# Two stacked transformer blocks: stage ends by token tile, the root mean square on products, and unrolled layers

## The reference

```python
def first_block(x, c, ...):
    for l in range(2):
        sh1, sc1, gt1, sh2, sc2, gt2 = split(silu(c) @ w_ada[l] + b_ada[l], 6)
        u = x * (1 + sc1) + sh1
        y = mixer(u, ...)                   # w_in, attention, convolution, gates, w_out
        x = layer_norm(ALPHA * x + (1 + gt1) * y, ln_mix_g[l], ln_mix_b[l])
        u = x * (1 + sc2) + sh2
        h = square(relu(u @ w_up[l])) @ w_down[l]
        x = layer_norm(ALPHA * x + (1 + gt2) * h, ln_ffn_g[l], ln_ffn_b[l])

def second_block(x, ...):
    for l in range(2):
        h = rmsnorm(x, ln_mix_g[l])
        proj = h @ w_in[l]                  # three kinds of attention: ya, yb, yc
        gates = sigmoid(h @ w_gate[l] + b_gate[l])
        x = x + (gates[0] * (ya @ w_br_a) + gates[1] * (yb @ w_br_b) + gates[2] * (yc @ w_br_c)) @ w_o[l]
        h = rmsnorm(x, ln_ffn_g[l])
        x = x + (silu(h @ w_ffn_gate[l]) * (h @ w_ffn_up[l])) @ w_ffn_down[l]
    return rmsnorm(x, final_norm_g)
```

## Time and profile before

| | before |
|---|---|
| median of 3 runs | 2055.03 us (2049.10 to 2055.74) |
| span of the profiled execution, first to last instruction | 2034.9 us |
| TensorE busy | 1834.9 us, 90% |
| VectorE busy | 1293.3 us, 64% |
| ScalarE busy | 868.6 us, 43% |
| GpSimd busy | 48.1 us, 2% |
| DMA | 345.85 MB, mean 170 GB/s |

### The profile page before, as it was taken

How to read it: one execution, slowest core, us unless ns; L and a number is a source line. 1 busy time by engine, 2 the same in 40 slices (tenths; PEclk the granted TensorE clock), 3 DMA queues, 4 the chain that set the end, 5 groups by cost and what they waited for, 6 DMA issues and landing times.

```text
span 2034.9 us, 29393 instructions
## 1 busy us (share of the span) xinstructions
PE 1834.9 (90%) x8402; PEld 1439.7 (71%) x8402; DVE 1293.3 (64%) x2005; ACT 868.6 (43%) x1463; POOL 48.1 (2%) x96
## 2 busy tenths in 40 slices
PE   5698997999698997999499999899989999989997
PEld 2385576777475576777399777688869977768886
DVE  3468987556668986555445688645544568864554
ACT  1244333444243343444145566434435556643443
POOL 0000000000100000000100000000000000000000
PEclk9799998999799998999799999999999999999999
DMA  7675554656375544555266533445555653345553
GB/s 234 240 247 165 166 166 153 199 186 211 122 233 159 165 156 165 186 196 175 84 212 189 172 122 105 155 154 179 179 184 170 189 174 119 104 155 156 180 178 116
DMA packets 210879, 345.85 MB, mean 170 GB/s; under 512 B 20104, under 2 KB 95798, under 8 KB 210530
## 3 DMA queue, kind: packets, MB, share of 16 engines
q1 hardware_dynamic: 208756, 337.79, 52.1%
q0 software_dynamic: 2032, 6.97, 1.1%
HBM read 343.62 MB, written 1.07 MB: 169 GB/s over the span
## 4 chain that ended last, share of the span: by engine, by line
issue 50%; POOLq 1%; POOL 0%; DVE 0%
POOLq L1463 0%; POOL x_rstd L1464 0%; POOLq L1471 0%; DVE x_res L1668 0%; POOLq L1478 0%; POOLq L1298 0%; POOL sub_rstd L1464 0%; POOL lat_rstd L1464 0%; POOLq L1469 0%; POOLq L1474 0%; POOL gates L1457 0%; POOLq L1476 0%; POOLq L352 0%
## 5 line engine op out<-in xcount | busy, mean ns | idle before, releaser
L125 DVE TENSOR_TENSOR w_lo_b<-w_raw_b,w_hi_b 128x1024 fp32r<-128x1024 f32 (+3 forms) x336 | 363.0, 1101 | 195.2 <-ACT w_hi_b L119 193.2
L119 ACT CAST w_hi_b<-w_raw_b 128x1024 fp32r<-128x1024 f32 (+3 forms) x336 | 314.0, 951 | 177.2 <-PE acc_b L146 79.9
L119 ACT CAST w_hi_a<-w_raw_a 128x1024 fp32r<-128x1024 f32 x232 | 241.6, 1049 | 246.9 <-PE prod_a L146 127.2
L144 PE MATMUL prod_b<-w_hi_b,hT_hi 128*128 128x512 f32 (+1 forms) x912 | 340.5, 373 | 6.5 <-DVE hT_lo L207 3.7
L125 DVE TENSOR_TENSOR w_lo_a<-w_raw_a,w_hi_a 128x1024 fp32r<-128x1024 f32 x232 | 277.5, 1222 | 97.6 <-ACT w_hi_a L119 96.8
L146 PE MATMUL prod_b<-w_hi_b,hT_lo 128*128 128x512 f32 (+1 forms) x912 | 334.6, 367 | 0.0
L145 PE MATMUL prod_b<-w_lo_b,hT_hi 128*128 128x512 f32 (+1 forms) x912 | 333.8, 366 | 0.0
L144 PE MATMUL prod_a<-w_hi_a,uT_hi 128*128 128x512 f32 x592 | 243.4, 411 | 12.9 <-DVE uT_lo L207 7.0
L146 PE MATMUL prod_a<-w_hi_a,uT_lo 128*128 128x512 f32 x592 | 237.5, 401 | 0.0
L145 PE MATMUL prod_a<-w_lo_a,uT_hi 128*128 128x512 f32 x592 | 237.5, 401 | 0.0
L144 PEld LDWEIGHTS prod_b<-w_hi_b,hT_hi 128*128 128x128 f32 x912 | 173.2, 190 | 34.0 <-issue 5.8
(11 more groups left out here) (308 smaller groups left out, 2511.2 us busy)
## 6 DMA issues: line engine op xcount, KB each, us to landing
w_raw_a<-in_w_in_dram SPq DMA_DIRECT2D x72, 512.0 KB, 3.8
w_raw_b<-in_w_in_dram SPq DMA_DIRECT2D x192, 172.0 KB, 2.4
ada_raw<-in_w_ada_dram SPq DMA_DIRECT2D x64, 512.0 KB, 5.9
w_raw_a<-in_w_up_dram SPq DMA_DIRECT2D x64, 512.0 KB, 4.5
w_raw_a<-in_w_down_dram SPq DMA_DIRECT2D x64, 512.0 KB, 5.4
w_raw_b<-in_w_gate_dram SPq DMA_DIRECT2D x96, 256.0 KB, 3.0
w_raw_b<-in_w_ffn_gate_dram SPq DMA_DIRECT2D x88, 256.0 KB, 3.5
w_raw_b<-in_w_ffn_up_dram SPq DMA_DIRECT2D x88, 256.0 KB, 4.2
```

What stands on the lines that cost most here:

```text
L119: act.copy(self.hi[:, s, 0:cols], self.raw[:, s, 0:cols]).then_inc(self.hi_done, 1)
L125: dve.tensor_tensor(self.lo[:, s, 0:cols], self.raw[:, s, 0:cols], self.hi[:, s, 0:cols].bitcast(F32), ALU.subtract).then_inc(self.lo_done, 1)
L144: pe.matmul(out, a_hi, w_hi, start=first and c == 0, stop=False)
```

## The change

- **Tile by tile at stage ends.** A new method `part` multiplies a weight group against one token tile. The last four groups of w_out and w_o, and the last down products of both feed-forwards, run for token tile 0 first, then for tile 1. New semaphores (`down0_done`) tell VectorE that tile 0 of a down product is complete.
- **Half rows.** Residual and norm go by token tile and by half rows of 512 columns; u_ready, u2_ready and h_ready count four halves for two tiles. Transposes of a half start when that half is there.
- **Transposes between parts.** `turned_tile` runs the first weight tile of a stage tile by tile, with the turns of the later halves between its groups. In block 2 the first two turns of the next stage stand between the last parts of the stage before.
- **Block 1, next layer.** The norm's gain and shift are folded into the next layer's modulation, so u comes straight from the statistics. x itself is normed after the low parts of u.
- **Block 2.** x is multiplied by the gain alone; the reciprocal root is applied to the products (`take_scaled`, the gate sum, the tanh, and for the hidden rows half the root and its square). ScalarE's squares move behind the last high part, and ScalarE and VectorE wait for the root before they touch products.
- **Layers unrolled.** All loops over layers are loops of the program that writes the kernel; loops over weight tiles stay.

```diff
+    def part(self, pe, pos, lhs, k0, width, chunks, tok, out, first, last, tile_end=True):
+        s = pos.slot(RING)
+        lhs_hi, lhs_lo = lhs
+        if tok == 0:
+            pe.wait_ge(self.lo_done, pos.count(RING + 1))
+        for c in range(chunks):
...
+        if last and tile_end and tok == 0:
+            mm.then_inc(self.tile0_done, 1)
+        if tok == TOKS - 1:
+            mm.then_inc(self.used, 1)
+        return mm
...
+    def turned_tile(self, pe, pos, lhs, width, outs, turn, taken, vacant=None):
+        turn(0)
+        for tok, out in enumerate(outs):
+            if vacant:
+                vacant(tok)
+            for g in range(4):
+                if g % 2 == 0:
+                    taken(2 * tok + g // 2)
+                self.part(pe, pos + g, lhs, KG * g, width, KG, tok, out, g == 0, g == 3)
+                if g == 0:
+                    turn(2 * tok + 1)
+                if g == 2 and tok == 0:
+                    turn(2)
...
-            with dve.Fori(0, LAYERS) as l:
+            for l in range(LAYERS):
...
+                if l == 0:
+                    for tok in range(TOKS):
+                        for h in range(2):
+                            modulated(tok, h)
+                    for n in range(4):
+                        split(layer(l, n, G1), 1)
+                        take_u_lo(n)
+                else:
+                    last_residual(0, 0)
+                    last_residual(0, 1)
+                    split(layer(l, 0, G1), 1)
+                    last_residual(1, 0)
+                    next_u(0, 0)
+                    next_u(0, 1)
+                    take_u_lo(0)
+                    last_residual(1, 1)
+                    split(layer(l, 1, G1), 2)
+                    take_u_lo(1)
+                    next_u(1, 0)
+                    split(layer(l, 3, G1), 1)
+                    take_u_lo(2)
+                    next_u(1, 1)
+                    take_u_lo(3)
+                    for tok in range(TOKS):
+                        dve.drain()
+                        normed(x_res[:, tok, :], x_res[:, tok, :], tok, ln_vec[:, 0, :], ln_vec[:, 1, :]).then_inc(x_ready, 1)
                 dve.memset(gate1_acc, 0.0)
...
+                mix_residual(0, 0)
+                mix_residual(0, 1)
+                split(layer(l, at + 8, G1), 1)
+                mix_residual(1, 0)
+                next_u2(0, 0)
+                next_u2(0, 1)
+                take_u2_lo(0)
+                mix_residual(1, 1)
+                split(layer(l, at + 9, G1), 2)
+                take_u2_lo(1)
+                next_u2(1, 0)
+                split(layer(l, at + 11, G1), 1)
+                take_u2_lo(2)
+                next_u2(1, 1)
+                take_u2_lo(3)
...
+                if l < LAYERS - 1:
+                    shift1, scale1 = (ada_first[:, l + 1, v, :] for v in range(2))
+                    dve.scalar_tensor_tensor(u_rows[:, 1, :], scale1, 1.0, ln_vec[:, 1, :], ALU.add, ALU.mult)
+                    dve.scalar_tensor_tensor(scale1, scale1, 1.0, ln_vec[:, 0, :], ALU.add, ALU.mult)
+                    dve.drain()
+                    dve.tensor_tensor(shift1, shift1, u_rows[:, 1, :], ALU.add)
+                    dve.drain()
...
+                for tok in range(TOKS):
+                    for i, (j, g) in enumerate(OUT_ORDER[4:8]):
+                        W.part(pe, layer(l, at + 4 + i, G1), uT, KG * g, NT, KG, tok, (outs, late)[j][tok], False, g == 3)
...
+            def take_scaled(tile, last_group, outs, cols):
+                for tok, out in enumerate(outs):
+                    W.wait_tile(act, tok, tile, last_group)
+                    act.activation(out, prod[tok][:, 0:cols], ACT.Copy, scale=x_rstd[:, 0, tok:tok + 1])\
+                       .then_inc(prod_free[tok], 1)
...
+                split(layer(l, 3, G2), 1, KG * IN2_W)
+                take_h_hi(3)
+                for tok in range(TOKS):
+                    square_x(2 * l, tok)
+                act.wait_ge(x_rstd_done, layer(l, TOKS - 1, 2 * TOKS).count(1))
...
+            def gained(tok, j, out, g, ready):
+                cols = slice(j * NT, (j + 1) * NT)
+                dve.tensor_tensor(out[:, tok, cols], x_res[:, tok, cols], g[:, cols], ALU.mult).then_inc(ready, 1)
...
+                second_u(0, 0)
+                second_u(0, 1)
+                split(layer(l, G2_FF, G2), 1)
+                take_u2_lo(0)
+                take_u2_lo(1)
+                second_u(1, 0)
+                split(layer(l, G2_FF + 1, G2), 1)
+                second_u(1, 1)
+                dve.drain().then_inc(vec_free, 1)
+                split(layer(l, G2_FF + 2, G2), 1)
+                take_u2_lo(2)
+                split(layer(l, G2_FF + 3, G2), 1)
+                take_u2_lo(3)
+                dve.wait_ge(x_rstd_done, layer(l, 2 * TOKS - 1, 2 * TOKS).count(1))
...
+                        W.part(pe, layer(l, G2_O + 4 + i, G2), uT, KG * g, NT, KG, tok, (late, early)[j][tok], False, g == 3)
+                        if tok == 1 and i == 1:
+                            u2_turn(0)
+                        if tok == 1 and i == 2:
+                            u2_turn(1)
...
+                down_part(0, 0, 0)
+                down_part(0, 1, 0)
+                down_part(0, 0, 1)
+                hidden_turn(nt, layer(l, F2 - 2, F2))
+                T.taken(pe, layer(l, F2 - 2, F2))
+                down_part(1, 0, 0).then_inc(down0_done, 1)
+                down_part(1, 1, 0).then_inc(down0_done, 1)
+                down_part(0, 1, 1)
+                T.taken(pe, layer(l, F2 - 1, F2))
+                down_part(1, 0, 1)
+                if l < LAYERS - 1:
+                    next_turn = lambda n: rows_turn(layer(l + 1, n, F2), h_rows[:, n // 2, :], 4 * (n % 2))
+                    for n in range(2):
+                        pe.wait_ge(h_ready, layer(l + 1, n, 4).count(1))
+                        next_turn(n)
+                down_part(1, 1, 1)
```

More of the change, by code:

```diff
@@ L60, in __init__ @@
     def __init__(self, k, *regs):
-        self.k, self.regs = k, regs
+        self.k = k + sum(r * step for r, step in regs if isinstance(r, int))
+        self.regs = tuple((r, step) for r, step in regs if not isinstance(r, int))
     def __add__(self, j):
@@ L469, in _ @@
             load_constants(sp)
-            with sp.Fori(0, LAYERS) as l:
-                ls = bass.ds(l, 1)
+            for l in range(LAYERS):
+                ls = slice(l, l + 1)
                 w_in, w_up, w_down = dr["w_in"][ls], dr["w_up"][ls], dr["w_down"][ls]
@@ L1038, in _ @@
             bias_rows.multiply(pe, prod[0])
-            with pe.Fori(0, LAYERS) as l:
+            for l in range(LAYERS):
                 pe.wait_ge(c_ready, 1)
@@ L1947, in rows_turn, with turned_tile @@
                                  for c in range(n)])
+            def turned_tile(pos, width, banks, turn, taken, vacant=None):
+                for tok in range(TOKS):
+                    if vacant:
+                        vacant(tok)
+                    for g in range(4):
+                        if g % 2 == 0:
+                            taken(2 * tok + g // 2)
+                        W.part(pe, pos + g, uT, KG * g, width, KG, tok, banks[tok], g == 0, g == 3)
+                        if tok == 0 and g < 2:
+                            turn(2 + g)
             def qk_turns(n, fill):
@@ L2111, in step @@
                     down(at + 4, lhs, fill, first, False)
-                for g in range(4):
-                    W.multiply(pe, layer(l, G2_FF + g, G2), uT, KG * g, NT, KG, late, g == 0, g == 3)
+                turned_tile(layer(l, G2_FF, G2), NT, late, u2_turn, lambda n: T.taken(pe, layer(l, F2_U2 + n, F2)))
                 for e in range(2):
```

359 lines of the change are left out of this document (208 added, 151 removed).

## The result

| | before | after |
|---|---|---|
| median beside each other | 2053.20 us (4 runs, 2049.10 to 2055.74) | 1990.37 us (4 runs, 1985.32 to 1992.42) |
| ratio, 95% interval | | 0.9705 (0.9679 to 0.9732) |
| profiled execution: span, mean granted clock | 2034.9 us, 0.959 | 1989.5 us, 0.974 |
| time of that execution | not listed | 1991.26 us |

The change makes the kernel 2.9% faster. The two spans differ by 45.4 us, where the sum had 46.0. So the sum and the predicted time have to be judged apart.

The account below looks back on a forecast made before the run. TensorE, busy 90% of the span, stands still at stage ends behind a VectorE chain. Terms summed to -46.0 us, taking the span from 2034.9 to 1988.9; plus 20.1 around it, 2009 us, range 1994 to 2029.

Parts of the forecast that it names:

- the stall: At block 2's layer turn: VectorE idles 4.42 us ending in "issue"; unrolling removes it; end worth 9.5 us, 6.5 otherwise.
- Mixer to feed-forward, block 1: Gap between w_out and feed-forward, both layers: tile-wise order starts the first matmuls earlier, 5.5 us won each (3 to 6.5).
- my queue: Each engine's work listed in the new order with today's durations, giving the forecast start and end times of tiles.
- Layer 0 to 1, block 1: Layer turn: tile 15 us earlier, 4.4 lost to delayed norm, 2 to clock; 8 us won (5 to 12).
- Start of block 1: First weight tile: alternating splits and low parts wait for transposes, costing 4.4 us (3 to 5.5).
- block 2: Mixer to feed-forward wins 8.5 us twice (6.5 to 9.5), layer turn 9.5 (7 to 11); root leaves the path.
- Block 1 to 2: Entry of the second block: residuals and norm earlier, second tile still waiting for its weight; 3.2 us won (1.5 to 6.4).
- The end: End of the kernel: TensorE ends 0.5 us earlier, norm of tile 0 ready sooner; 1.7 us won (1 to 3).
- (a): Rival, chance 0.15: each handover round inside first tiles costs 0.8 us more, 19 us in all, giving 2028 us.
- (b): Rival, chance 0.10: clock holds at shorter gaps and a second-tile stall in layer 1 hides; 61 us won, 1994 us.
- (c): Rival, chance 0.05: first tiles full of holes stay at 1.2 GHz throughout, costing 59 us, giving 2068 us.
- (d): Rival, chance 0.03: no change, since the next stages' products run into weights that come no earlier.

## Why the forecast was wrong, and where it was right

**The step that failed is the last one of the sum.** "The median of the runs, 2055.0, stands 20.1 above the span; launch and end are not touched, so 2009 us." What lies around a span is 2.0 us for before and 1.8 for after. The other 18 us were the distance between one short execution and the medians of other executions, and I carried them over to a kernel that need not have them. Of the 18, 8 to 10 are how far the recorded span lies under the usual one of the later groups; the rest is that the runs of before in the first result were longer than those of every later group, for a reason that no run shows. The changed kernel had no such distance: the profiled execution of after took 1991.26 us and its median is 1990.37. With 2 us the same sum gives 1990.9, and its ends (61 and 28 us) 1976 and 2009, which hold the time.

**That the sum met the two spans to 0.6 us is in part luck.** Medians side by side on one chip say 59.1, not 45.4: the recorded execution of before, at a clock of 0.959, was shorter than its usual ones by 8 to 10 us, and that of after longer than the later ones by some 4. By medians block 1 gave 19.5 (17.8 in the sum: +4.4 - 11.0 - 8.0 - 3.2), block 2 gave 20.3 (25.2: 17.0, 6.5 without the stall, 1.7), and unrolling 14.7 where I had the 3 of the stall. So two terms were mis-sized and cancelled in part: unrolling by 12 too little, block 2 by 5 too much. "The one stall of that kind that I name" overlooked one: the trace of before has a second "issue" stall of VectorE, 1.96 us in front of 533.91, at the layer turn of block 1, and the run with the loops of block 1 unrolled doesn't have it. For block 2 the traces show each end at its forecast (8.9, 9.1, 9.1 and 1.6) and then 1.3 and 1.1 us given back in the stages behind them; that what is won at an end isn't all kept stood in none of my terms. (The 9.1 of the layer turn has the unrolling in it; against the kernel with unrolling alone it is 6.1.)

**Mixer to feed-forward, block 1** (5.5; measured 7.5 and 6.8). Mechanism right, though one reading of today's gap was wrong: by VectorE's timeline two of the "four residual halves" are done before 309.7, so the gap holds two. Moved by the 3.3 us that the kernel is late here, my queue had the first transposes at 315.3, the first matmul at 318.1 and the tile's end at 334.8; the trace has 315.04, 317.17 and an end 1.5 us earlier. The two waits for turned rows inside the tile hardly showed, and the half microsecond that I took off for the clock was not lost: the gap itself runs at 1.00, and the tile behind it at 0.89 against 0.84 in the earlier trace rows, so the clock did fall, but for less time.

**Layer 0 to 1, block 1** (8; 11). The norm in front of the split stands where forecast (540), with TensorE waiting 4.56 us for a forecast 4.4. The 3 us more are the first tile, which was through at 537.8 where the queue, moved by the same 3.3 us, had 540.2 to 541.1. The forecast's own numbers (15 less 4.4 less 2) give 8.6, not 8. And 1.9 to 2.4 us of the 11 are the turn of the loop: the kernel with unrolling alone has them, and from it to the kernel with block 1 changed this end gives 8.0.

**Start of block 1** (+4.4; +5.1) and **block 2** (8.5, 9.5; 9.0, 9.1): right, with the holes, the missing gap and the missing "issue" wait as described. At the layer turn of block 2 the second tile waits for the root, as forecast.

**Block 1 to 2** (3.2; 1.5, the lower end). The wait for the second tile's weight came as described, 4.49 us on ScalarE, and the clock fell in it (0.85). The second tile starts 3.0 us earlier where the queue had 3.6, and 1.5 of that go to the low clock; the price that I allowed for it, 0.4, was too small. That the new order wins anything here isn't shown: the kernel with unrolling alone is already 3.2 us ahead at this place.

**The end** (1.7; 1.6): right.

**Rivals.** (a) costly handovers: fell, the first tiles were quicker than my queue. (b) The clock does not fall at the shorter gaps: true in block 2, where the granted clock is 1.00 from 1014 to 1984 us, through all three handovers; in block 1 the first tile still has 0.89. The row that was to speak for (b), 169.6 to 174.7 at 1.00, stops just short: behind that gap the trace of before has 0.57 from 174.7 to 178.7. The Trainium skill, TensorE: Matmul & The Clock Gate, Part 4: PE-mode transpose, says that transposes don't count as busy in the same way; no stretch here has transposes for long enough to test it, and with matmuls around them the clock stayed up in block 2. (c) No first tile was under 0.7 throughout. (d) Late weights cost one place, not all. The Trainium skill, Runtime: NRT & Kernel Launch, section Instruction fetch mechanics, by which a taken branch to a target outside the window held forces a fetch, agrees with both turns in sign; the runs give the sizes, 2.85 and 1.99 us. That the stalls are fetches isn't shown, only that they go with the loop.

## What to carry to other kernels

Never turn a summed span into a time by adding the distance from a single profiled execution to the median: take what lies around the span from an execution that has both, and compare medians with medians. Where an engine's chain fills the gap between two stages, running the last and first matmuls row tile by row tile took gaps of 14.7 and 23.6 us down to 4.1 and closed those of 11.4 and 13.8. Put each operation that is pushed back behind the split that the next tile wants, and look at the stretch behind as well: what is won there can be lost to weights that now land late. And price unrolled loops apart from the rest: it was a quarter of the gain here.

## What the runs showed of the hardware

- What lies around a span: 1.97 to 2.08 us for before in 39 executions, and 1.99 to 3.21 in ten more (eight of them under 2.1); 1.75 to 1.82 for after (8).
- The same kernel with the same matmuls had 1834.9 us of busy TensorE at a mean clock of 0.959 and 1844.5 at 0.953: 39 of its executions scatter over 18 us. The eight of the changed kernel scatter over 7, too few to say that it scatters less.
- A turn of a layer loop stalled VectorE for 2.85 us in block 2 and 1.99 us in block 1 beyond what its operands needed.
- With matmuls and transposes alternating and holes of up to 1.8 us, TensorE kept 1.00 through the stage ends of block 2, which had 0.70 and 0.66 before; gaps of 4.1 us still cost some of the clock behind them (0.89).
- With the first tile behind the layer turn of block 1 freed from VectorE's wait (6.2 us won), ScalarE waited 4.82 us for a weight soon after, and 4.8 us of the gain were lost again.
- What stays open: where the rest of the 14.7 us of unrolling comes from (the traces show about 2 at one turn and 3 to 4 at the other), what takes back the 4 us won at the start of block 1, and why the four runs of before beside the first result (2049 to 2056) are longer than those of the later groups (medians 2044.6 to 2046.5).
